# Experts of a mixture layer: GpSimd halves chunks in every other slot only, and the extra slots stand between the experts' own

## What is computed

```python
def run(args):                      # a block of tokens and its expert
    xb, e = args
    gate, up = jnp.split(xb @ w_gate_up[e], 2, axis=-1)
    return (jax.nn.silu(gate) * up) @ w_down[e]
```

## Time and profile before

| what | before |
|---|---|
| three runs | 3014.64, 3019.86, 3019.99 us (median 3019.86) |
| the profiled execution | 3016.14 us, of which the span in the profile is 3014.4 |
| mean granted clock of TensorE in it | 0.913 of full speed |
| busy over the span | PE 2526.9, DVE 1706.9, ACT 1293.1, POOL 899.2 us |
| experts' stage, first to last tanh | 2552.45 to 2971.66 us of the span |

### The profile page before, as it was taken

The page is one execution under the profiler, slowest core; times in us unless marked ns, Lnnn a source line. Parts: engine busy times, 40 slices in busy tenths (PEclk is TensorE's granted clock), DMA queues, the critical chain, the costliest instruction groups (busy, mean ns, idle before and its releaser), DMA issues.

```text
span 3014.4 us, 40303 instructions
## 1 busy us (share of the span) xinstructions
PE 2526.9 (84%) x16787; PEld 2235.4 (74%) x16787; DVE 1706.9 (57%) x2615; ACT 1293.1 (43%) x2032; POOL 899.2 (30%) x527
## 2 busy tenths in 40 slices
PE   4999987898977679999999595677898873888884
PEld 4999986888877678898898493566766663667673
DVE  3454436777751246666656534685556514777785
ACT  3444333333321245655565323333344213777774
POOL 1111213343421122222222212301300012888883
PEclk8999996999998889999999698888789976999997
DMA  3223210000005122222221220313310432888822
GB/s 131 86 87 122 85 46 13 26 13 25 13 4 145 30 64 71 71 71 74 71 69 49 67 76 24 95 46 74 99 43 25 129 108 102 296 315 300 303 80 84
DMA packets 227328, 273.83 MB, mean 91 GB/s; under 512 B 42680, under 2 KB 193817, under 8 KB 214602
## 3 DMA queue, kind: packets, MB, share of 16 engines
q1 hardware_dynamic: 212634, 262.81, 27.9%
q0 software_dynamic: 14512, 8.45, 0.9%
HBM read 281.41 MB, written 31.05 MB: 104 GB/s over the span
## 4 chain that ended last, share of the span: by engine, by line
PE 59%; DVE 17%; ACT 13%; POOL 6%; issue 2%; DMA 2%; SPq 1%; DVEq 0%; POOLq 0%; ACTq 0%
PE ps L93 17%; PE ps L95 16%; PE ps L94 16%; POOL wlo L103 3%; ACT whi L99 2%; POOL ex_lo L103 2%; ACT sp L107 2%; DVE wlo L103 2%; PE ps L770 1%; PE ps L1339 1%; PE ps L432 1%; ACT xTh L99 1%; DVE p L1534 1%; DVE work L1977 1%; ACT ex_hi L99 1%
## 5 line engine op out<-in xcount | busy, mean ns | idle before, releaser
L93 PE MATMUL ps<-hn_h,whi 128*128 128x264 f32 (+2 forms) x2328 | 720.5, 310 | 63.0 <-POOL wlo L103 30.9
L94 PE MATMUL ps<-hn_l,whi 128*128 128x264 f32 (+2 forms) x2328 | 703.1, 302 | 0.0
L95 PE MATMUL ps<-hn_h,wlo 128*128 128x264 f32 (+2 forms) x2328 | 702.1, 302 | 0.0
L93 PEld LDWEIGHTS ps<-hn_h,whi 128*128 128x128 f32 x2328 | 448.6, 193 | 96.9 <-issue 30.5
L95 PEld LDWEIGHTS ps<-hn_h,wlo 128*128 128x128 f32 x2328 | 447.9, 192 | 14.9
L94 PEld LDWEIGHTS ps<-hn_l,whi 128*128 128x128 f32 x2328 | 448.5, 193 | 11.3
L103 POOL TENSOR_TENSOR wlo<-wraw,whi 128x2048 fp32r<-128x2048 f32 (+1 forms) x55 | 206.7, 3759 | 716.2 <-ACT whi L99 716.2
L103 DVE TENSOR_TENSOR wlo<-wraw,whi 128x2048 fp32r<-128x2048 f32 (+2 forms) x116 | 245.3, 2114 | 200.9 <-ACT whi L99 200.3
L99 ACT ACTIVATE whi<-wraw 128x2048 fp32r<-128x2048 f32 (+1 forms) x171 | 268.9, 1574 | 71.1 <-PE ps L95 51.6
L660 DVE SCALAR_TENSOR_TENSOR c<-ub,vec,c 128x528 f32<-128x528 f32 x48 | 46.0, 959 | 145.8 <-ACT c L107 145.8
L107 ACT ACTIVATE ub<-ps,vec 128x528 f32<-128x528 f32 x48 | 33.7, 702 | 166.2 <-PE ps L95 166.2
(11 more groups left out here) (618 smaller groups left out, 7052.8 us busy)
## 6 DMA issues: line engine op xcount, KB each, us to landing
wraw<-in_w_gate_up SPq DMA_DIRECT2D x33, 1024.0 KB, 7.3
wraw<-in_hy_w_in SPq DMA_DIRECT2D x32, 1024.0 KB, 5.8
wraw<-in_da_w_in SPq DMA_DIRECT2D x64, 512.0 KB, 4.3
ex_raw<-in_w_gate_up SPq DMA_DIRECT2D x31, 1024.0 KB, 7.5
ex_raw<-in_w_down SPq DMA_DIRECT2D x16, 1024.0 KB, 7.3
wraw<-in_w_down SPq DMA_DIRECT2D x16, 1024.0 KB, 7.2
wraw<-in_w_in SPq DMA_DIRECT2D x14, 1024.0 KB, 5.5
wraw<-in_hy_w_out SPq DMA_DIRECT2D x8, 1024.0 KB, 7.1
```

What stands on the lines that cost most here:

```text
L93: e.matmul(out, lhsT=l[0], rhs=r[0], start=start, stop=False)
L94: e.matmul(out, lhsT=l[0], rhs=r[1], start=False, stop=False)
L95: return e.matmul(out, lhsT=l[1], rhs=r[0], start=False, stop=stop)
```

## The change

The order of slots becomes a table SLOTS. Position n of the loop now holds the slot SLOTS[n]: 0, 1, 2, 32, 3, 4, 5, 6, 7, 33, 8 and so on; the extra slots stand at positions 3, 9, 15, 20, 26, 31 and 37, and the last position, 38, is expert 31. In the experts' part GpSimd makes the low part of gu(n,0) of every even position n, where it isn't gathered, and no other: 18 of them (positions 20 and 26 are gathered), one of which, gu(0,0), it made before, too. All other low parts are DVE's. Weights, tokens, results and arithmetic are the same.

```diff
+    SLOTS = sorted(range(NB), key=lambda x: (x + 0.5) / 32 if x < 32 else (x - 32 + 0.75) / NX)
+
-    def experts(x, g):
+    def experts(n, g):
+        x = SLOTS[n]
         k = 4 if g < 2 else 2
...
+    even_slots = [first["gu", n, 0] for n in range(0, NB, 2)]
...
     def lo_by(i):
-        return ("w.lo.pool", i) if i % 3 == 0 and not gathered(i) else ("w.lo.vec", i)
+
+        pool = i in even_slots if i >= EX else i % 3 == 0
+        return ("w.lo.pool", i) if pool and not gathered(i) else ("w.lo.vec", i)
...
-        e.indirect_dma_start(xg[n % 3][:], None, hnd, bass.IndirectOffsetOnAxis(tok[:, n:n + 1], 0), bounds_check=L - 1,
+        e.indirect_dma_start(xg[n % 3][:], None, hnd, bass.IndirectOffsetOnAxis(tok[:, SLOTS[n]:SLOTS[n] + 1], 0), bounds_check=L - 1,
...
-        e.indirect_dma_start(yd, bass.IndirectOffsetOnAxis(dst[:, n:n + 1], 0), ys[n % 2][:], None, bounds_check=2 * L - 1,
+        e.indirect_dma_start(yd, bass.IndirectOffsetOnAxis(dst[:, SLOTS[n]:SLOTS[n] + 1], 0), ys[n % 2][:], None, bounds_check=2 * L - 1,
...
-            act(e, ys[n % 2][:, 512 * g:512 * g + 512], bank[6 + g], ACT.Copy, scale=tq[:, n, 1:2]).then_inc(*mark("mo.act", "y", n, g))
+            act(e, ys[n % 2][:, 512 * g:512 * g + 512], bank[6 + g], ACT.Copy, scale=tq[:, SLOTS[n], 1:2]).then_inc(*mark("mo.act", "y", n, g))
```

## The result

The changed kernel is **slower**: 3037.82 us as the median of 6 runs (3027.91 to 3044.67), against 3015.89 of 6 runs of the kernel before (3014.06 to 3019.99); the ratio is 1.0068, with a 95% interval of 1.0049 to 1.0086. That is 21.9 us more, where 37 were forecast: the time came out 19 us under the 3057 that was given.

The account below looks back on a forecast made before the run. A ring through GpSimd's low part, for which PE waits 1.4 us, was taken to set 11.17 us a slot. 351.9 + 5.1 + 34.2 + 33.5 + 23.8 = 448.5 against 411.3 gave 3057 us, range 3010 to 3085.

Parts of the forecast that it names:

- (4): In the experts' part, PE's waits for late token rows: nine ordinary ones, 34.2 us; five behind two gathers, 33.5 us.
- step (6): Extra slots: moving their gathers, fetches and scatters costs nothing beyond fetch waits; missing weights give DMA engines room.
- (1): Net 14 low parts go from GpSimd to DVE, hidden under PE in an all-DVE slot of 9.51 us.
- (2): GpSimd's low part ends 4.40 us behind DVE's, slightly later than PE wants it: 17 x 0.3 = 5.1 us.
- Step (3): Fetch issued at T + 3.05 behind two weight transfers, landing T + 9.5; PE waits 3.8 us once in two slots.
- T: End of GpSimd's low part in a slot, forecast at 9.65 us after PE's start of the slot.
- Step (5): PE's clock: halved for 3.4 us behind each of 14 waits, 23.8 us; bounds nothing and 3.4 each.
- The faster one: Fetch not behind the weights: DMA queues take turns, 2996 us, chance 0.10; or issue takes 1 us, 2995, 0.06.
- DVE becomes the bound: DVE a further 1 us late in slots with GpSimd's low part, or waits at upper bounds: 3074 to 3081, chance 0.09.
- The case in between: PE's waits for token rows stand at their lower bound: 3034 us, or 3011 without the clock's price; chance 0.17.

Follow-up runs that it names:

- experiment 9: Changed kernel with no low part on GpSimd in the experts' part but the first, DVE making the others, new slot order: 2956.53 us, ratio 0.98.
- Experiments 1: Changed kernel with the fetch of n+2 moved ahead of GpSimd's low part and the two gathers: 3003.7 us, ratio 0.9943.
- experiment 5: Changed kernel where SP holds back the weights of gu(m,0), m even from 4, until the token rows of position m-1 have landed: 2990.84 us, ratio 0.9916.
- experiment 6: Changed kernel where, in the nine ordinary cases, DVE's low part waits until GpSimd has issued the fetch: 2994.81 us, ratio 0.9942.
- Experiment 7: Changed kernel with extra slots' weight gathers going into buffers nobody reads, and ACT not waiting for them: 3055.87 us, ratio 1.0147.
- 8: Changed kernel with the fetch and the gathers of an extra slot's weights both ahead of GpSimd's low part: 2997.36 us, ratio 0.9934.
- experiment 2: Changed kernel with only the new slot order, GpSimd keeping the low part of every third chunk as before: 3020.16 us, ratio 1.0001.
- experiment 4: Changed kernel with 24 useless transposes on PE ahead of each wait for an odd position's token rows: 3030.64 us, ratio 1.005.
- experiment 10: Changed kernel with no low part on GpSimd in the experts' part but the first, and the old slot order: 2963.61 us, ratio 0.9827.

## Why the prediction was wrong in size, and where it was right

The direction and the mechanism were right. The step that failed is (4), for the five fetches behind gathers: it had 33.5 us for their waits, and they measured 14.4. Two smaller misses: step (6) had nothing for positions 20 and 26, which waited 3.3 us, and the 3.8 us that the sum put on top for the median weren't there, since the median of six runs of the kernel before is 3015.89 us, 0.3 below the profiled one.

Term by term, between the marks, in us:

| term | forecast | measured |
|---|---|---|
| 37 slots without a wait | 351.9 | 351.9 (9.51 in the before; 9.52 in experiment 9) |
| nine ordinary waits for token rows | 34.2 | 33.0 (2.9 to 4.6 each) |
| five with an extra slot | 33.5 | 14.4 (2.5 to 3.3) |
| at positions 20 and 26 | 0 | 3.3 (1.6 and 1.7) |
| GpSimd's low part later than wanted, and the clock | 5.1 + 23.8 | 31.4, the rest |
| sum | 448.5 | 434.0 |

*Steps (1) and (2)*, the low parts: right. A slot with GpSimd's low part and no other wait takes 9.70, 0.19 over 9.51 (0.3 forecast). The low part took 4.93 us, not 4.60, with DVE's turn in front of it.

*Step (3)*, the fetch: right in every part. It is issued at T + 3.04, weights are ahead of it, and PE waits for it; PE goes on 8.9 to 10.5 us behind T, where T + 9.5 was forecast. Experiments 1, 5 and 6 each take away one link (the place in GpSimd's order, the weights ahead, DVE's turn), and each takes the ordinary waits away. None of the three changes what is computed. The changed kernel has a check of its own: for n = 17 and 23 the fetch is issued as late, 3.05 us behind the low part, SP has no weights to issue there, and PE doesn't wait.

*Step (4)* failed. "The fetch at 7.95, just behind the weights of gu(n+4,0), issued at T + 7.0": those weights were not issued then. They wait for a low part, and this for the high part of gu(n+2,0), which here is the gathered chunk of the extra slot itself, so ACT has to wait for its landing. The gather is behind GpSimd's low part and two weight transfers, and lands at T + 8.8:

```profile
2646.01 1.91 ACT L99 ACTIVATE ex_hi<-wraw 128x2048 fp32r<-128x2048 f32 x1 [5.96 <-DMA wraw<-in_w_gate_up,slot_rows]
```

(changed kernel, timeline of ACT), and SP issues those weights 4 us behind the landing, at 2650.28, when the fetch (issued by 2644.54) has landed (by 2646.38, where PE goes on):

```profile
2650.28 0.33 SPq L285 DMA_DIRECT2D wraw<-in_w_gate_up  x1
```

I had costed the gathers as time of GpSimd's, and not asked who waits for what they bring. One late transfer hid another: the wait of ACT lies beside PE's wait for the fetch. Experiment 7, without ACT's wait, has four of the five at 6.6 to 6.9 us; at position 3 the fetch is ahead of those weights there, too. Its 449.3 us beside the forecast's 448.5 are in part luck: it also has 3.8 us at positions 20 and 26 that the forecast lacks, and 4.0 us less at position 3.

At positions 20 and 26 the fetch itself stands behind two gathers (issued by 2773.74, where the gathers start at 2767.60 and 2769.79). These waits stay without ACT's wait (experiment 7) and are gone in the two runs that have the fetch ahead of the gathers (1 and 8), but also where GpSimd makes other low parts or none (2 and 9). Step (6) looked at GpSimd's time in such slots and not at the fetch's place behind the gathers; whether that place alone makes the waits isn't shown.

*Step (5)*, the clock: right in kind. 0.50 and 0.57 behind two of the waits (changed kernel):

```profile
2672.00:2675.40 3.40, 3.40 (x12) 3.02 (x13) 1.38 (x2) 2.05 (x3) 0.00 (x0) 0.50 0.92 370
...
2698.60:2702.00 3.40, 3.40 (x13) 3.08 (x14) 1.38 (x2) 2.04 (x3) 0.00 (x0) 0.57 0.38 141
```

Its size comes out of the pairs of slots. For a fetched position n I take the time of the slots n-1 and n from their tanh marks, less 2 x 9.51 us and the wait in it (in experiment 4 also less 2.6 us for the transposes, which is what they add in a slot without a wait). What is left over in all pairs of a kind:

| left over in | changed kernel | experiment 4, clock whole |
|---|---|---|
| nine ordinary pairs | 20.7 | 5.1 us |
| the pair of position 3 | 1.7 | 0.3 us |
| four pairs with the other odd extra slots | 7.9 | 7.9 us |

So the low clock costs 1.7 us in each of the nine, as forecast, 17 us in all with position 3, and nothing in the four others. There experiment 4 has PE wait 0.7 to 0.8 us for DVE's gate, which stands behind ACT's late high part. Experiment 7, with the low clock and without ACT's wait, has 8.3 us left over in these four: either alone costs that much, and both together no more. The forecast had counted 6.8 us of clock for them.

*Step (6)*, the extra slots: the last slots' 11.2 us did go, but the order alone is worth nothing where GpSimd has low parts (experiment 2), because gathers then stand in front of them.

*The rivals.* The faster one fell in both halves: the fetch does stand behind the weights (experiment 5), and its issue is held (experiment 6). "DVE becomes the bound" fell most plainly: DVE makes all low parts in experiment 9 and PE has no gap. The case in between had its upper end, 3034, near the result, but that is luck. It had every wait short, and nine had their full size; the five that were short were so for a reason that it didn't name.

What stays open: why single ordinary waits run from 2.9 to 4.6 us, since the changed kernel's trace has no landing times of fetches in this stretch.

## What to carry to other kernels

Where a step is moved in an engine's order, look past its own wait to what is queued behind it: here the low part could wait, and the small fetch behind it could not. A small transfer that is needed soon should be issued ahead of whatever frees the buffers of large ones. And before work is balanced between two engines that block each other, try it all on the faster one: it cost nothing here, and GpSimd's help cost 52 us in the kernel before (experiment 10) and 81 in the changed one (experiment 9).

## What was not expected of the hardware

- An expert's transfers need less than the share suggests. At 11.17 us a slot the DMA engines were 0.85 busy over 250 us and 0.88 in the 50 us of the earlier trace rows, which I read as 9.8 us of work; at 9.51 us a slot they are 0.90 busy (8.6 us) and nobody waits.
- GpSimd's low part ends 4.50 us behind the DVE low part that it had to let go first (2661.52 against 2657.02), close to the 4.40 read before. That is a little less than the 4.60 us that it takes where DVE's doesn't run before it; why isn't shown.
